# A two-layer hybrid backbone step: order of the first transfers, conditioning matmuls, and the GLA output's matmul order

## What is computed

```python
mod = (silu(cond) @ w_mod + b_mod)[:, None, :]
sh1, sc1, g1, sh2, sc2, g2 = split(mod, 6)
h = rmsnorm(x, norm1_g) * (1.0 + sc1) + sh1
proj = h @ w_in          # gq gk gv gg glr cu dq dk dv gates
# three branches: GLA (linear attention with decay, both directions),
# a 31-tap convolution, differential attention
merged = ga * (o_gla @ wb1) + gb * (o_conv @ wb2) + gc * (o_diff @ wb3)
x = x + g1 * (merged @ w_out)
h2 = rmsnorm(x, norm2_g) * (1.0 + sc2) + sh2
a, b = split(h2 @ w_ffn_in, 2)
x = x + g2 * ((silu(a) * b) @ w_ffn_out)
```

## Time and profile before

| | before |
|---|---|
| runs | 1468.16, 1471.8, 1472.45 us |
| median | 1471.8 us |
| profiled execution | 1473.47 us, span of its instructions 1471.7 us |
| TensorE busy, mean granted clock | 97% of the span, 0.991 |
| VectorE, ScalarE, GpSimd busy | 52%, 41%, 47% |
| bytes moved | 208.65 MB, mean 142 GB/s |

### The profile page before, as it was taken

The page is one execution under the profiler, slowest core; times in us unless marked ns, Lnnn a source line. Parts: engine busy times, 40 slices in busy tenths (PEclk is TensorE's granted clock), DMA queues, the critical chain, the costliest instruction groups (busy, mean ns, idle before and its releaser), DMA issues.

```text
span 1471.7 us, 22482 instructions
## 1 busy us (share of the span) xinstructions
PE 1424.8 (97%) x9083; PEld 1343.5 (91%) x9083; DVE 765.9 (52%) x992; ACT 603.8 (41%) x836; POOL 697.2 (47%) x296
## 2 busy tenths in 40 slices
PE   6999999999999999999999999999999999999998
PEld 3788999998998999999979889999989999999998
DVE  4359877986774212120254697689858442211012
ACT  3453434545634333332235433455455343333321
POOL 1244443444463555555524434344535645555552
PEclk9999999999999999999999999999999999999999
DMA  8846233433542655553326643243326434344342
GB/s 312 296 150 227 73 102 92 115 100 101 173 157 92 219 172 176 172 200 120 127 77 193 219 130 101 73 119 102 101 94 206 130 115 134 124 129 129 119 125 72
DMA packets 163311, 208.65 MB, mean 142 GB/s; under 512 B 9228, under 2 KB 135176, under 8 KB 163208
## 3 DMA queue, kind: packets, MB, share of 16 engines
q1 hardware_dynamic: 162656, 207.00, 43.9%
q10 hardware_dynamic: 552, 0.22, 0.1%
HBM read 204.05 MB, written 3.15 MB: 141 GB/s over the span
## 4 chain that ended last, share of the span: by engine, by line
PE 80%; DVE 10%; ACT 4%; DMA 2%; issue 2%; POOL 1%; SPq 0%; DVEq 0%; ACTq 0%; POOLq 0%
PE ps L733 23%; PE ps L735 22%; PE ps L734 22%; PE ps L645 2%; ACT w_hi L1220 1%; DVE gates L1946 1%; PE ps L827 1%; DVE t L1609 1%; PE ps L777 1%; DVE fac L1784 1%; PE ps L778 1%; PE ps L779 1%; DMA w_raw<-in_w_in_dram 1%; POOL w_lo L606 1%; DVE h_lo L1950 1%
## 5 line engine op out<-in xcount | busy, mean ns | idle before, releaser
L606 POOL TENSOR_TENSOR w_lo<-w_raw,w_hi 128x1024 fp32r<-128x1024 f32 x288 | 693.7, 2410 | 751.7 <-ACT w_hi L1220 566.0
L733 PE MATMUL ps<-h_hi,w_hi 128*128 128x384 f32 x1600 | 552.0, 345 | 6.9 <-DVE h_lo L1615 4.2
L734 PE MATMUL ps<-h_lo,w_hi 128*128 128x384 f32 x1600 | 539.1, 337 | 0.0
L735 PE MATMUL ps<-h_hi,w_lo 128*128 128x384 f32 x1600 | 538.8, 337 | 0.0
L1220 ACT ACTIVATE w_hi<-w_raw 128x1024 fp32r<-128x1024 f32 x200 | 208.5, 1044 | 452.9 <-PE ps L735 302.0
L733 PEld LDWEIGHTS ps<-h_hi,w_hi 128*128 128x128 f32 x1600 | 303.3, 190 | 27.9 <-issue 17.6
L734 PEld LDWEIGHTS ps<-h_lo,w_hi 128*128 128x128 f32 x1600 | 303.8, 190 | 1.4
L735 PEld LDWEIGHTS ps<-h_hi,w_lo 128*128 128x128 f32 x1600 | 303.3, 190 | 0.0
L1650 DVE SCALAR_TENSOR_TENSOR conv_acc<-conv_in,cw,conv_acc 128x399 f32<-128x399 f32 x240 | 213.1, 950 | 1.8
L1512 ACT ACTIVATE w_hi<-w_raw 128x1024 fp32r<-128x1024 f32 x88 | 93.2, 1061 | 231.1 <-PE ps L735 183.5
L1970 DVE TENSOR_TENSOR sq<-sq,ps 128x768 f32<-128x768 f32 x22 | 21.0, 954 | 260.9 <-PE ps L735 260.9
(11 more groups left out here) (258 smaller groups left out, 1648.4 us busy)
## 6 DMA issues: line engine op xcount, KB each, us to landing
w_raw<-in_w_in_dram SPq DMA_DIRECT2D x112, 512.0 KB, 3.6
w_raw<-in_w_ffn_in_dram SPq DMA_DIRECT2D x88, 512.0 KB, 3.5
mod_late<-in_w_mod_dram SPq DMA_DIRECT2D x56, 512.0 KB, 5.4
w_raw<-in_w_ffn_out_dram SPq DMA_DIRECT2D x44, 512.0 KB, 3.7
mod_early<-in_w_mod_dram SPq DMA_DIRECT2D x32, 512.0 KB, 5.8
w_raw<-in_w_branch_dram SPq DMA_DIRECT2D x24, 512.0 KB, 3.4
w_raw<-in_w_out_dram SPq DMA_DIRECT2D x16, 512.0 KB, 3.3
mod_second<-in_w_mod_dram SPq DMA_DIRECT2D x8, 512.0 KB, 11.0
```

The lines of the kernel that those rows point to most:

```text
L606: nc.gpsimd.tensor_tensor(m["w_lo"][:, n % SPL, cols], m["w_raw"][:, n % RAW, cols], m["w_hi"][:, n % SPL, cols].bitcast(F32), ALU.subtrac ...
L733: mm(out, hi[:, at:at + P], rhs[0][:, k, :], start=start, stop=False)
L734: mm(out, hi[:, at:at + P], rhs[1][:, k, :], start=False, stop=False)
L735: ins = mm(out, lo[:, at:at + P], rhs[0][:, k, :], start=False, stop=stop)
```

## The change

1. SP issues the token stage first, then pieces 0 to 3 of half 0, the first input piece, pieces 4 to 6, and piece 7 of half 0 into a ninth slot of `mod_second`. The `wa` transfers move from piece 0 to piece 2; the first gate piece from 4 to 5.
2. TensorE transposes before the first step; the square sums come two steps earlier. ScalarE loads the table for ln and exp at once after the first sigmoid, and takes the first input piece between squares 5 and 6.
3. Steps 0 to 2 of half 1 stand ahead of the first input piece, 3 and 4 after its row tile 0, 5 and 6 after row tile 1, 7 after row tile 2; the turn follows the piece.
4. ScalarE takes the fifth input piece ahead of the last two high parts.
5. In the FFN of layer 0 the 16 steps stand in fours after rounds 2, 4, 6 and 8.
6. `gla_out` does its five 128-row products first, then the four 64-row ones.
7. `SQUARE_ACT`, `LEVEL_TAPS` and `STATE_TAPS` move one square and two taps.

```diff
-SECOND_AT = [-1, -1, -1, -1, -1, 0, 0, 0]
-GATE_LOAD = [4, 5, 5, 5, 6, 7, 8, 8]
+SECOND_AT = [-1, -1, -1, 99, 99, 99, 99, 99]
+GATE_LOAD = [5, 5, 5, 5, 6, 7, 8, 8]
...
-SQUARE_ACT = [32, 34, 35, 36]
+SQUARE_ACT = [31, 34, 35, 36]
...
-LEVEL_TAPS = [1, 2, 8, 7, 4, 5, 7]
-STATE_TAPS = 16
+LEVEL_TAPS = [0, 2, 8, 7, 4, 7, 7]
+STATE_TAPS = 15
...
+SECOND_IN = {0: (3, 4), 1: (5, 6), 2: (7,)}
+FIRST_PIECE_AT = 4
+FIRST_SUMS = {3: (3,), 4: (4, 5), 5: (6, 7)}
...
-            for i in range(KD):
-                if i == 2:
-                    sp.dma_start(m["stage"][:, 0, :], x_prompt[0]).then_inc(first_in.sem, 16)
-                    sp.dma_start(m["stage"][:, 1:3, :], x_sample[0].rearrange("(t p) d -> p t d", p=P)
-                                 ).then_inc(first_in.sem, 16)
+            sp.dma_start(m["stage"][:, 0, :], x_prompt[0]).then_inc(first_in.sem, 16)
+            sp.dma_start(m["stage"][:, 1:3, :], x_sample[0].rearrange("(t p) d -> p t d", p=P)).then_inc(first_in.sem, 16)
+            for i in range(KD - 1):
+                if i == FIRST_PIECE_AT:
+                    first_piece()
                 mod_late(i)
+            dst, src = paired_columns(m["mod_second"][:, KD, :], KD - 1, 0)
+            sp.dma_start(dst, src).then_inc(second_full[KD].sem, 16)
...
+                            if l == 0 and s == 0 and j in SECOND_IN:
+                                for kk in SECOND_IN[j]:
+                                    mod_mm(0, 1, kk)
...
-                    mm(ps[:, bank, 0:P], v[:, 0, cols], att[:, 0, hh, :], start=True, stop=True)
-                    o = ps[:, bank, P:2 * P]
...
+                    for tt in (1, 2):
+                        mm(outs[tt], v[:, tt, cols], att[:, tt, hh, :], start=False, stop=False, skip_group_check=True)
+                        mm(outs[tt], v[:, 3 - tt, cols], cr[:, 2 - tt, hh, :], start=False, stop=False, skip_group_check=True)
+                    for tt in (1, 2):
...
+                        mm(outs[tt], s0[rows, 0, hh // 2, :], q0, start=False, stop=False, skip_group_check=True)
+                        ins = mm(outs[tt], s0[rows, 1, hh // 2, :], q1, start=False, stop=True, skip_group_check=True)
...
-                            if half_chunk % 2 and 1 <= i <= KD:
-                                n = 2 * (i - 1) + half_chunk // 2
-                                mod_mm(l + 1, n // KD, n % KD)
+                            if half_chunk == 3 and i in (2, 4, 6, 8):
+                                for n in range(2 * i - 4, 2 * i):
+                                    mod_mm(l + 1, n // KD, n % KD)
...
             for k in range(KD):
+                if k == 6:
+                    act.wait_ge(raw_full[0].sem, 16)
+                    act.wait_ge(piece_used.sem, SPL)
+                    fn(m["w_hi"][:, 0, :], m["w_raw"][:, 0, :], ACT.Copy).then_inc(hi_ready.sem, 1)
                 square(0, 0, k)
-            act.preload_act_table_set(LN_EXP)
...
-                h_high(0, range(4, KD))
+                h_high(0, range(4, 6))
+                high(SPL)
+                h_high(0, range(6, KD))
```

More of the change, by code:

```diff
@@ L222, in memory @@
     over("conv_s", [P, CT, T], conv)
-    over("mod_second", [P, KD, D], gla)
-    assert KD * D * 4 <= 6 * H * T * 4
+    over("mod_second", [P, KD + 1, D], gla)
+    assert (KD + 1) * D * 4 <= 6 * H * T * 4
     prefix = own("prefix", [P, 2, 2, NT, P + 1])
@@ L295, in program @@
         late_used = signal("late_used")
-        second_full = [signal(f"second_full{i}") for i in range(KD)]
+        second_full = [signal(f"second_full{i}") for i in range(KD + 1)]
         second_used = signal("second_used")
@@ L420, in keys_of @@
             return P if q == 0 else T
-        late_pieces = ([(0, vec, k) for vec in (0, 2) for k in range(KD)] + [(0, 5, k) for k in range(KD)]
+        late_pieces = ([(0, 0, k) for k in range(KD - 1)] + [(0, 2, k) for k in range(KD)] + [(0, 5, k) for k in range(KD)]
                        + [(1, vec, k) for vec in (0, 1, 2) for k in range(KD)] + [(1, 5, k) for k in range(KD)])
@@ L501, in _ @@
                     col, width = IN_CHUNKS[chunk]
-                    piece(s, w_in[l, half * 512:(half + 1) * 512, col:col + width])
+                    if l or s:
+                        piece(s, w_in[l, half * 512:(half + 1) * 512, col:col + width])
                     for k in range(KD):
@@ L519, in _ @@
                             mod_early(early_at[l, 3, 0] + i)
-                    if s == 0:
+                    if s == 2:
                         sp.wait_ge(start_v.sem, 4)
@@ L534, in _ @@
                     if s == 6:
-                        sp.wait_ge(second_used.sem, KD)
+                        sp.wait_ge(second_used.sem, KD + 1)
                         for d in range(2):
@@ L636, in mod_mm @@
                     w, taken = m["mod_early"][:, i % EARLY, :], early_used
-                elif (layer, vec) == (0, 1):
-                    pe.wait_ge(second_full[k].sem, 16)
-                    w, taken = m["mod_second"][:, k, :], second_used
+                elif (layer, vec) == (0, 1) or (layer, vec, k) == (0, 0, KD - 1):
+                    i = k if vec else KD
+                    pe.wait_ge(second_full[i].sem, 16)
+                    w, taken = m["mod_second"][:, i, :], second_used
                 else:
@@ L703, in _ @@
             pe.wait_ge(start_v.sem, 7)
+            pe.wait_ge(first_in.sem, 32)
+            for kk in range(KD):
+                if kk >= 4:
+                    pe.wait_ge(x_ready.sem, kk - 3)
+                for tt in range(NT):
+                    ins = nc.tensor.transpose(ps[:, kk % 4, tt * P:tt * P + P],
+                                              m["stage"][:, tt, kk * P:kk * P + P], ident[:])
+                ins.then_inc(start_p.sem, 1)
             for k in range(KD):
                 mod_mm(0, 0, k)
[L706 to L715, removed]
+                if k == 2:
                     pe.wait_ge(x_ready.sem, KD)
-                if k >= 5:
-                    for kk in {5: (3,), 6: (4, 5), 7: (6, 7)}[k]:
+                if k in FIRST_SUMS:
+                    for kk in FIRST_SUMS[k]:
                         square_sum(0, 0, kk)
@@ L992, in _ @@
                             mod_mm(0, 1, k)
-                            if k == KD - 1:
-                                mod_turn(0, 1)
+                    if l == 0 and s == 0:
+                        mod_turn(0, 1)
                     for k in range(KD):
@@ L1182, in _ @@
             fn(m["csil"][:], ps[:, 7, T:T + 16], ACT.Sigmoid).then_inc(start_a.sem, 1)
+            act.preload_act_table_set(LN_EXP)
             def small_rows(l):
@@ L1366, in _ @@
                 flat_t = m["t"][:].rearrange("p a b -> p (a b)")
-                high(0)
-                if l == 0:
+                if l:
+                    high(0)
+                else:
                     inverse_rms(0)
@@ L1383, in _ @@
                             evacuate(c)
-                    if s != DECAY_ACT:
+                    if s not in (SPL, DECAY_ACT):
                         high(s)
@@ L1575, in mod_take @@
                     dve.wait_ge(early_used.sem, early_at[layer, vec, KD - 1] + 1)
-                elif (layer, vec) == (0, 1):
-                    dve.wait_ge(second_used.sem, KD)
+                elif layer == 0 and vec < 2:
+                    dve.wait_ge(second_used.sem, KD * vec + 1)
                 else:
```

19 lines of the change are left out of this document (10 added, 9 removed).

## The result

| | before | after |
|---|---|---|
| median of the runs beside each other | 1472.07 us (1468.16 to 1472.45) | 1460.36 us (1458.48 to 1460.64) |
| ratio, 95% interval | | 0.9925 [0.9912, 0.9938] |
| profiled execution, its span | 1473.47, 1471.7 us | 1460.64, 1458.8 us |
| mean granted clock | 0.991 | 0.995 |

The change is faster by 11.7 us, by 11.0 ± 1.9 if one goes by the ratio. Page, part 1, of the kernel after: busy time, share, instructions of each engine.

A forecast was written before the change was run, and what follows sets the result against it. TensorE was taken to bound the kernel. Terms 2.7 (opening) + 4.2 (fours) + 3.2 (GLA rows) = 10.1 us took the profiled 1473.47 to 1463.4; with runs' median 1.7 lower, 1462, range 1457 to 1467.

The forecast's parts named there:

- steps 4 and 5: Layer 0 FFN's conditioning steps in fours save 4.2 us; GLA output products ordered by rows save 3.2 us.
- steps 1 and 2: Opening: reordered transfers land the stage at 9.3; second-half pieces between row tiles bring the second norm 2.4 us forward.
- step 3: Opening: fifth input piece's split inside the second norm lets that piece start at once, 2.7 us gained, nothing for the clock.
- The opening's term: Opening, transfers, row tiles and fifth split together: 2.7 us gained, bounds 1.0 to 5.5 us.
- the two readings of rows 9: GLA heads: row changes cost 0.10 to 0.11 each, saving 3.2 us (taken), or 64-row products cost 0.32 themselves, saving 1.6.
- Small moves: Two convolution taps and one square moved: all at nothing, bounds −1 to +2 us.
- B: 64-row products cost by themselves and part of the FFN switch stays: 7.2 us gained, 1464.6; 10%.
- D: Slower: the clock falls after each longer stretch of partial tiles, four fours and eight heads; 1482; 3%.
- E: Nothing arrives: switch prices are hidden in how matmul ends are modelled, the opening gives 1 to 2 us; 1470; 4%.
- A: The opening gives nothing: low parts late by a second lock of 2.4 us, or a piece lands later; 1464.4; 15%.
- C: The opening gives more: clock kept and one lock less, 5.5 us; 1458.9; 12%.

The follow-up runs named there:

- opening alone: The kernel after with single steps in the FFN, the old `gla_out` and the old tables put back; 1467.92 us beside 1471.61, ratio 0.9974.
- fours alone: The kernel before with only layer 1's conditioning steps put in fours; 1467.3 us beside 1470.6, ratio 0.9969.
- late split: The kernel after with the fifth piece's high part back behind all high parts of the norm, both layers; 1461.48 us, ratio 0.9929; later 1461.13, 0.9926.
- rows alone: The kernel before with only the new order of products in `gla_out`; 1469.08 us beside 1470.6, ratio 0.9989.

## Why the prediction came out right

The forecast was 1462.0, range 1457 to 1467; measured 1460.36, and 1461.88 and 1459.84 in the later comparisons. The sum was 10.1 us; the ratios give 10.4 to 11.8. The mechanisms of steps 4 and 5 hold as they were worked out. In the opening the mechanism holds too, but that its figure is near is partly luck: earlier landings and a clock that stayed up, neither of them forecast, stand against a loss in layer 1 that was not forecast either.

1. **Landings (steps 1 and 2).** The order was right, and everything came 0.9 to 1.7 us earlier than forecast: the stage at 8.29 (forecast 9.3), the norm 25.04 (25.9), first low part at 26.85 (28.5), first input piece 28.66 (29.9), the end of the turn 37.31 (38.8), the second norm 38.20 (39.5). The step that missed is the landing of the pieces: by equal bytes the first one of half 1 was to be taken at 26.03 still, and TensorE took it at 24.66 (24.5 to 25.6 in the ten traces with the new order, 25.0 to 26.0 in the four with the old). For the stage itself one cause offers itself, that SP issues it sooner. After:

```profile
2.38 0.43 SPq L495
```

It begins at 2.38, before at 3.44, 1.06 later. TensorE took the stage 12.28 − 8.29 = 3.99 earlier, and 3.99 − 1.06 is two pieces of 1.46. But the fit proves nothing: at 3.44 the queues still had the two pieces ahead to move (TensorE waited for the first until 5.76), and over the fourteen traces the stage was taken at 8.2 to 9.3 in the new order and 11.4 to 12.3 in the old, a spread as large as the miss. From 3 to 11 us the queues moved 366 GB/s after and 345 before, 0.17 MB more, which is some 0.5 us of the 1.4 by which the first piece of half 1 came earlier. Why the rest came earlier was not tested; that the two `wa` transfers no longer stand ahead of half 1 is one candidate.

2. **Fifth piece (step 3).** Forecast 49.3, measured 48.03. The stretch from the second norm to it was forecast at 9.8 us and took 9.83; the miss is the norm's start, and so the landings and the clock. In the kernel with the early split in layer 0 only, whose layer 0 is the same, the fifth piece came at 49.22, with a clock of 0.67 instead of 0.90 from 30 to 35 us, under the row tiles: near the forecast, but by two misses that cancel. From the first input piece to the turn the forecast had counted 8.5 us, the kernel after took 8.51, and this one 9.45. The lock inside the norm was there once, at its price (2.78 for a pair of low parts that take 0.75). The Trainium skill, SBUF — State Buffer, section "Who interferes with whom", says that the ports that the two engines share are an exclusive lock, which the one that issues first holds for its whole instruction; the trace agrees. One reading of step 3 was wrong: TensorE did not wait "about as long as before" for low parts ahead of the fifth piece, but 1.6 us (the two waits shown under the opening), where the profile of before names no such wait.

3. **The clock (step 3).** I credited nothing. Here it stayed up behind the fifth piece, and from z to the keys too, where the kernel before lost about as much again. Windows of before and of after, from z to the keys:

```profile
62.80:177.90 115.10, 112.06 (x922) 100.77 (x922) 90.32 (x107) 51.83 (x67) 49.23 (x20) 0.97 0.53 174
```

```profile
57.30:170.20 112.90, 108.95 (x922) 97.83 (x922) 89.99 (x105) 51.80 (x67) 48.93 (x20) 1.00 0.54 176
```

The same 922 matmuls take 3.1 us less of TensorE, of which TensorE then waits 0.9 more (3.95 against 3.04 idle): the stretch is 2.2 shorter. So in the profiled pair the opening gives 5.5 at z (3.7 by the second norm's start, 0.2 by the split's place, 1.6 by the clock), and 2.2 behind it. The medians give 3.8. That not each execution of before loses the clock and not each of after keeps it is the likely reason: behind z it was 1.00 in one of the four old openings too, and 0.985 instead of 1.00 in two of the ten new ones. But there is one trace per comparison and kernel, so it isn't shown.

4. **What was missed: layer 1.** `high(SPL)` stands in a function that both layers run, and my count looked at layer 0 alone. In layer 1 the fifth piece is not late, its early split only pushes two splits into the norm: two locks, 5.37 us for low parts of 1.59, of which TensorE sees 1.0. The opening's term, 2.7, measured 3.8 [2.4, 5.3] in the opening alone. The trace of that kernel doesn't show the loss in layer 1; the three of the kernel after do.

5. **Fours.** 4.2 forecast; 4.3 to 4.4 in every trace, 4.6 [2.5, 6.5] by the times. The price of a four, 2.07 us, was exact in all four of them, the clock stayed up, and SP's longest waits in the stretch are the same as before (17.0 us for a split, 8.6 for a step).

6. **GLA output.** 3.2 forecast; 3.0 to 3.2 in the traces, 1.6 [−0.3, 3.4] by the times. The choice between the two readings of rows 9 was right. The Trainium skill, TensorEngine Tiling, section "Key Properties", says that changing the tiling mode drains the array and changing only the tile doesn't; the trace agrees, with 0.22 and 0.23 us inside the run of 64-row products and 0.31 to 0.33 at its edges.

7. **Small moves.** Nothing forecast; 0.3 to 0.6 in one comparison, not told from zero. What rows 10 show has moved: without its tap VectorE waits 2.35 at the first product, and with two taps more in front it waits nothing at the second.

```profile
103.73 2.65 DVE L1810 TENSOR_TENSOR fac<-fac,gqk 128x1536 f32<-128x1536 f32 x1 [2.35 <-ACT fac L1322]
...
164.25 1.41 DVE L1808 TENSOR_TENSOR fac<-fac,gqk 128x512 f32<-128x512 f32 x2
```

Of the rivals, B fell by the spacing inside the run of four and D by the window of the four. E fell by the fours alone and the rows' traces. A and C: by the trace the kept clock of C came true in layer 0 and the second lock of A in layer 1; in the medians neither of them shows alone.

What stays open: what decides whether the clock falls behind a gap; whether the row tiles between the steps pay in the whole; why the pieces landed earlier; why the opening's gain is 5.4 at z in its own trace and 3.8 in the medians, for which the spread of both openings (z at 60.9 to 62.8 and 57.3 to 58.5) is a likely but not a shown cause.

## What to carry to other kernels

Count a move for each place where the moved line runs: an early weight split that closes a gap in the first layer cost 1.0 us of TensorE in the second, where no gap was, and guarding it with the layer's number gave the lowest mean. Before crediting a move with a later milestone, take the stretch from the last instruction that it can't have touched: the early split looked like 1.85 us and was 0.2, and the clock's part has to be counted apart. Partial matmuls (other rows or columns than their neighbours') cost by the entries and exits, about 0.2 us for each change of rows and 0.35 for entering and leaving one of 32 columns, so gather them; it is a gain that could be read here to 0.1 us from the spacing of starts. Where single terms are as small as the spread of executions, compare stretches between the same instructions in several traces.

## What the runs showed of the hardware

- A gap of 2.1 us on TensorE was followed by the lower clock (0.52 to 0.76 in the next windows) in four traces (before, fours alone, both with the late split) and by 1.00 in one (rows alone). In the last the clock had been at 0.50 from 30 to 35 us, in the four at 0.66, 1.00, 0.58 and 0.81. With 1.7 us of waits in parts of at most 1 us in its place it stayed at 1.00 in all eight traces. A fall can't be priced in by a gap alone.
- Two weight splits of GpSimd at 755.07 and 758.02, 0.28 us apart, held four low parts of VectorE for 5.37 us instead of 1.59, and lasted 2.67 and 2.52 themselves, where one that met a pair of low parts took 2.38 (28.74). One split costs a pair 2.0 to 2.1; the two together cost four 3.8.
- Four 64-row fp32 products of 128 columns in a row: 0.31, 0.33, 0.22, 0.23 and 0.31 us from start to start, entry and exit included.
